# A hybrid attention/mLSTM decoder step: the rotary product of the query heads taken from TensorE to VectorE and GpSimd

## The reference

```python
def partial_rope(x, pos):
    half = ROT_DIM // 2                      # ROT_DIM = 32, half = 16
    ang = pos[:, None] * inv[None, :]
    cos, sin = jnp.cos(ang)[:, None, :], jnp.sin(ang)[:, None, :]
    x1, x2 = xf[..., :half], xf[..., half:ROT_DIM]
    return jnp.concatenate([x1 * cos - x2 * sin, x2 * cos + x1 * sin, xf[..., ROT_DIM:]], axis=-1)

aq = partial_rope(rms_norm(aq.reshape(B, S, ATT_HEADS, ATT_HD), q_norm_w), pos)
ak = partial_rope(rms_norm(ak.reshape(B, S, ATT_HEADS, ATT_HD), k_norm_w), pos)
```

## Time and profile before

| | |
|---|---|
| median of 3 runs | 468.84 us (468.48 to 469.5) |
| the profiled execution | 469.01 us, span 466.9 us |
| PE / PEld busy | 455.6 us (98%) / 414.0 us (89%) |
| DVE / ACT / POOL busy | 393.8 us (84%) / 290.5 us (62%) / 100.5 us (22%) |
| DMA | 150.91 MB, mean 323 GB/s |
| query stage on PE | about 17 us to 48 us of the span |

### The profile page before, as it was taken

The page is one execution under the profiler, slowest core; times in us unless marked ns, Lnnn a source line. Parts: engine busy times, 40 slices in busy tenths (PEclk is TensorE's granted clock), DMA queues, the critical chain, the costliest instruction groups (busy, mean ns, idle before and its releaser), DMA issues.

```text
span 466.9 us, 11342 instructions
## 1 busy us (share of the span) xinstructions
PE 455.6 (98%) x3855; PEld 414.0 (89%) x3855; DVE 393.8 (84%) x1610; ACT 290.5 (62%) x487; POOL 100.5 (22%) x181
## 2 busy tenths in 40 slices
PE   6999999999999999999999999999999999999997
PEld 4899899897879789888899889889898899899997
DVE  4898899699999799999899999889999946568861
ACT  4866545676984496896485695667958346324430
POOL 2040421013323213422321242312222201000000
PEclk9999999999999999999999999999999999999999
DMA  8899699749999999999999999998999995447511
GB/s 306 324 355 406 173 349 363 237 156 336 320 416 408 388 360 352 412 412 408 409 384 297 405 413 409 411 384 285 403 415 410 409 382 182 162 149 261 181 49 48
DMA packets 44858, 150.91 MB, mean 323 GB/s; under 512 B 6192, under 2 KB 7796, under 8 KB 44672
## 3 DMA queue, kind: packets, MB, share of 16 engines
q1 hardware_dynamic: 20368, 70.77, 41.0%
q0 software_dynamic: 19008, 67.20, 37.4%
q10 hardware_dynamic: 5424, 12.21, 6.9%
HBM read 137.37 MB, written 12.76 MB: 322 GB/s over the span
## 4 chain that ended last, share of the span: by engine, by line
PE 66%; ACT 12%; DVE 9%; DMA 7%; issue 4%; ACTq 1%; SPq 0%; DVEq 0%; POOLq 0%
PE pj L545 25%; PE pj L548 12%; PE wk L545 8%; PE pa L728 4%; PE wk L548 4%; DMA kpages<-in_cache_k 4%; ACT whi L829 3%; DVE kpages L1181 2%; DMA out_C_s<-cslot 2%; ACT L849 2%; DVE wlo L1082 2%; DVE cslot L1263 1%; PE wk L498 1%; PE wk L650 1%; PE wk L684 1%
## 5 line engine op out<-in xcount | busy, mean ns | idle before, releaser
L545 PE MATMUL pj<-xn,whi 128*128 128x264 f32 x1328 | 180.8, 289 | 1.6 <-ACT mqT L987 1.3
L545 PEld LDWEIGHTS pj<-xn,whi 128*128 128x128 f32 x1328 | 168.5, 189 | 10.2 <-issue 6.2
L1082 DVE TENSOR_TENSOR wlo<-wraw,whi 128x1024 fp32r<-128x1024 f32 x112 | 136.2, 1219 | 9.5 <-ACT whi L829 9.1
L829 ACT ACTIVATE whi<-wraw 128x1024 fp32r<-128x1024 f32 x112 | 117.9, 1053 | 21.0 <-PE wk L548 13.5
L1181 DVE CUSTOM_DVE_ANT_0 kpages<-kpages,qbc 128x128 f32<-128x128 f32 x512 | 116.3, 292 | 3.5 <-DMA kpages<-in_cache_k 3.3
L548 PE MATMUL pj<-xn,wlo 128*128 128x264 f32 x664 | 93.9, 284 | 0.7 <-DVE wlo L1082 0.7
L548 PEld LDWEIGHTS pj<-xn,wlo 128*128 128x128 f32 x664 | 85.4, 188 | 1.1 <-DVE wlo L1082 1.1
L418 POOL DMA_DIRECT2D kpages<-in_cache_k x64 | 34.3, 536 | 167.4 <-DVE sco L1181 145.1
L418 POOL DMA_DIRECT2D vpages<-in_cache_v x64 | 33.9, 530 | 60.6 <-issue 38.4
L1181 DVE DVE_READ_ACCUMULATOR2_ANT sco<- 128x1 f32 x512 | 42.1, 82 | 0.0
L728 PE MATMUL pa<-vpages,prob 128*32 128x256 f32 x512 | 33.8, 384 | 1.9 <-ACT prob L887 1.9
(11 more groups left out here) (270 smaller groups left out, 609.5 us busy)
## 6 DMA issues: line engine op xcount, KB each, us to landing
wraw<-in_weights SPq DMA_DIRECT2D x112, 512.0 KB, 6.7
kpages<-in_cache_k POOLq DMA_DIRECT2D x64, 512.0 KB, 8.4
vpages<-in_cache_v POOLq DMA_DIRECT2D x64, 512.0 KB, 11.1
cslot<-in_states SPq DMA_DIRECT2D x16, 512.0 KB, 8.8
out_C_s<-cslot ACTq DMA_DIRECT2D x16, 512.0 KB, 8.1
xres<-in_tokens SPq DMA_DIRECT2D x1, 1056.0 KB, 5.6
out_k_p<-kT ACTq DMA_DIRECT2D x4, 256.0 KB, 10.0
out_v_p<-v_nat ACTq DMA_DIRECT2D x4, 256.0 KB, 5.1
```

Of the source, the lines that this page charges most:

```text
L545: mm(bank[:, 0:T], whi[:, q, k, :], src[:, g, k, :], start=(k == 0 and g == 0), stop=False)
L829: A(whi[:, n % WSPLIT], wraw[:, n % WRAW], ACT.Copy).then_inc(whi_ready, 1)
L1082: V.tensor_tensor(wlo[:, n % WRAW], wraw[:, n % WRAW], whi[:, n % WSPLIT], ALU.subtract).then_inc(wlo_ready, 1)
```

## The change

For the 8 query heads PE no longer multiplies with the permutation matrix. DVE swaps the two halves of the 32 rotated rows by a lane shuffle inside SBUF, multiplies them with the sine (whose sign now lies in the table), and adds the product of the head's 32 rows with the cosine, which POOL makes into `hT[:, 1]` and announces by the semaphore `scaled`. The last multiplication by 1/rms still runs over all 128 rows. Rows 32 to 127 are no longer touched by cosine and sum. The keys still go through `norm_sums` and `rope_norm`, with the sign moved from the matrix to the table.

POOL's stream is written in another order: the 11 pages are issued in twos between the eight cosine products, and the decay rows' write and read are placed behind the products of head 5 and head 6. PE's wait for the buffer pair is on `rs_ready` where it was on `q_ready`.

```diff
+SWAP = [(m + ROT // 2) % ROT for m in range(ROT)]
@@ gpsimd
-            pool.wait_ge(proj, 2)
-            for s in range(KSLOTS):
-                keys(s)
-            for s in range(VSLOTS - 1):
-                values(s)
-
-            pool.wait_ge(rows_ready, 1)
-            pool.dma_start(rows_dram, rows[:, :, :].rearrange("p a t -> p (a t)")).then_inc(row_put, 16)
-            pool.wait_ge(row_put, 16)
-            decay_rows(0)
+            pool.wait_ge(blank, 6)
+            pool.wait_ge(boot_r, 16)
+            for h in range(HEADS):
+
+                pool.wait_ge(evac, h + 1)
+                if h:
+                    pool.wait_ge(q_ready, h)
+                pool.tensor_tensor(hT[0:ROT, 1, :], qT[0:ROT, h, :], cos[0:ROT], ALU.mult).then_inc(scaled, 1)
+                if h in (1, 2):
+                    for s in range(KSLOTS // 2):
+                        keys(KSLOTS // 2 * (h - 1) + s)
+                if h in (3, 4, 5, 6):
+                    for s in range(2 * (h - 3), min(2 * (h - 2), VSLOTS - 1)):
+                        values(s)
+                if h == 5:
+                    pool.wait_ge(rows_ready, 1)
+                    pool.dma_start(rows_dram, rows[:, :, :].rearrange("p a t -> p (a t)")).then_inc(row_put, 16)
+                if h == 6:
+                    pool.wait_ge(row_put, 16)
+                    decay_rows(0)
             spread_rows(0)
@@ tensor
                     pe.wait_ge(evac, g + 1)
-                    if g == 0:
-                        pe.wait_ge(boot_r, 16)
                     if g >= 2:
-                        pe.wait_ge(q_ready, g - 1)
-                    norm_sums(wk[2 * (g % 2)], wk[2 * (g % 2) + 1], g % 2, qT[:, g, :])
+                        pe.wait_ge(rs_ready, g - 1)
+                    mm(wk[2 * (g % 2)][:, 0:T], ones, sq[:, g % 2, :], start=True, stop=True).then_inc(norm_ps, 1)
@@ vector
+            def rope_head(h):
+
+                x = qT[:, h, :]
+                ch.link(V.stream_shuffle(hT[0:ROT, 0, :], x[0:ROT], SWAP))
+                ch.step(V.tensor_tensor(hT[0:ROT, 0, :], hT[0:ROT, 0, :], sin[0:ROT], ALU.mult))
+                ch.join()
+                dve.wait_ge(scaled, h + 1)
+                ch.link(V.tensor_tensor(x[0:ROT], hT[0:ROT, 0, :], hT[0:ROT, 1, :], ALU.add))
+                dve.wait_ge(rs_ready, h + 1)
+                V.tensor_tensor(x, x, rs[:, h % 2, :], ALU.mult).then_inc(q_ready, 1)
@@
                 dve.wait_ge(boot_r, 16)
-                dve.wait_ge(norm_ps, h + 1)
-                dve.wait_ge(rs_ready, h + 1)
-                rope_norm(qT[:, h, :], rs[:, h % 2, :], wk[2 * (h % 2) + 1], q_ready)
+                dve.wait_ge(evac, h + 1)
+                rope_head(h)
@@ constants
-        c[m + half, C_ROT + m] = -1.0
+        c[m + half, C_ROT + m] = 1.0
-        c[s * half:(s + 1) * half, C_SIN:C_SIN + T] = np.sin(ang)
+        c[s * half:(s + 1) * half, C_SIN:C_SIN + T] = (2 * s - 1) * np.sin(ang)
```

More of the change, by code:

```diff
@@ L290, in build @@
         blank, blank_eye = sem("blank"), sem("blank_eye")
+        scaled = sem("scaled")
         xsq_act, xsq_dve, xn_ready = sem("xsq_act"), sem("xsq_dve"), sem("xn_ready")
```

## The result

The changed kernel takes 478.31 us (476.71 to 478.36, four runs) against 468.82 for the kernel before: 1.0196 times as long, 95% interval 1.0178 to 1.0213. The forecast was 474.4, range 469.3 to 478.5. The direction and the chain of waits held; the size was 9.5 us where 5.6 had been forecast. The time lies outside the forecast's own range, which ended at 476.3, and only 0.2 us inside the wider one, whose end was the price of rival 3.

A forecast was written before the change was run, and what follows sets the result against it. PE was taken to bound the query heads (98% busy, 3.81 us a head). Landing +4.0 and clock +1.6 gave +5.6 on 469.0, 474.6, less 0.2: 474.4 us; own range 469.3 to 476.3, wider to 478.5.

The forecast's parts named there:

- rival 3: Much slower: POOL's product near 2.4 us delays pages and the rows' write, +9.7 us, 478.5 us; chance 12%.
- The path: Before PE's transposes: rows' landing, two reads, last cosine product, sum and scaling in turn, transposes at 52.4 instead of 48.4.
- signs of being wrong: Rows landing in under 5 us, no PE wait before transposes, POOL products over 1.5 us, or body's end unmoved despite PE's pause.
- PE: Query heads on PE without permutation matmuls: period 3.36 us instead of 3.81, chunk 8 ending 3.15 us earlier, at 44.7.
- From landing to transposes: Behind the landing: reads 1.0 us, product 0.8, handovers 0.1, sum and scaling 0.43 each; landing 49.5, transposes 52.4.
- The landing itself: Decay rows' write on POOL's queue lands at 49.5 us, as late as before; bounds 45.0 and 51.2.
- 28.5 + 9 x 2.27: POOL's page queue: first page lands at 28.5, nine more 2.27 us apart, so the tenth at 48.9.
- its upper bound: POOL's page queue: weights' greater share slows a page to 2.46 us, so the rows land at 51.2.
- 22.6 + 4 x 3.36 + ...: POOL's stream: four head periods after head 0's end at 22.6; last page ahead issued 38.6, rows' write 39.4.
- the product: POOL's cosine product of a query head: 0.8 us, bounds 0.3 and 2.4, with room in the first heads.
- The clock: PE's clock falls in its 7.6 us pause before the transposes, making first matmuls slow: +1.6 us, bounds 0 and 2.
- The library: POOL's library choices before the products and the spreading: a long first call, about 6 us, given no more weight.

The follow-up runs named there:

- experiment 1: Changed kernel with the decay rows' write issued by ScalarE on its own queue after head 5: 469.80 us, ratio 1.0040 to the kernel before.
- experiment 6: Kernel before without PE's eight permutation matmuls of the query heads, queries left unrotated: 468.57 us, ratio 0.9991.
- experiment 8: Changed kernel with the cosine product made by DVE and POOL's stream as in the kernel before: 470.09 us, ratio 1.0031.
- experiment 11: Changed kernel with POOL's order and waits kept but no cosine products made: 474.84 us, ratio 1.0144.
- experiment 10: Changed kernel with rows' write on ScalarE's queue, reads behind all products, two product buffers, only seven pages between products: 470.31 us, ratio 1.0032.
- experiment 4: Changed kernel with 24 matmuls of zeros on PE before its wait for the last query head: 475.86 us, ratio 1.0161.
- experiment 12: Against the kernel before: DVE does the whole rotation, two heads a pass, no permutation matmuls on PE, rows' write on ScalarE's queue: 466.64 us, 0.9965.
- experiment 2: Changed kernel with the wait and reads of the decay rows behind all eight products, write still on POOL's queue: 475.24 us, ratio 1.0142.
- experiment 3: Changed kernel with the rows' write on ScalarE's queue and the wait and reads behind all cosine products: 470.47 us, ratio 1.0049.
- experiment 9: Changed kernel with the cosine product on DVE, POOL's stream as before, and rows' write on ScalarE's queue: 471.05 us, ratio 1.0057.

## Why the prediction was right, and where its size was off

**The path.** Right in every step from the landing on: the rows' landing, the reads, the product, the sum, the scaling and the transposes stand in the chain in that order, and experiment 1 gives 7.3 us of the loss back by moving one write to another queue. Of the prediction's signs of being wrong one came true as well: products on POOL over 1.5 us.

**PE.** Right: the heads stand 3.36 us apart, and chunk 8 ended at 45.2 where 44.7 was forecast.

**From landing to transposes.** Forecast 2.9 us, measured 57.03 - 53.93 = 3.1. The last product is 0.75 us for a forecast 0.8.

**The landing itself** is the term that was too small: 53.9 for 49.5. The forecast worked it out from the pages ahead of the write: the first lands at 28.5, nine more follow at 2.27 us each, the write 0.6 later. The time of the write's issue (39.4) does not enter; that the write took 10.2 us where 49.5 - 39.4 = 10.1 is a coincidence. What the changed kernel shows for the first page (issued at 24.94) and for the ninth and tenth together (issued at 42.6 and 43.2):

```profile
DMA to landing us min/median/max: 5.2/5.2/5.2
DMA to landing us min/median/max: 9.1/9.8/10.5
```

The first page landed at 30.1, the tenth at 53.7, the write 0.2 later. That is 2.62 us a page, and in the terms of the forecast +1.6 for the first page, +3.2 for the pace and -0.4 for the write. The step that failed is "28.5 + 9 x 2.27", above all the pace.

Two things made the pages slower, and no run tells their shares apart. One needs nothing of POOL's new stream: with the stream of before and PE's heads at 3.36 us, the eleven pages landed 2.46 us apart in experiment 6 and 2.59 in experiment 8, where the kernel before had 2.27, and the write landed at 51.7 and 52.4. The forecast had this as its upper bound (2.46 us a page, by the weights' greater share) and took the old pace all the same. The other is that the new stream gives the queue its pages too late to keep it full. The stretch of 32 to 36 us, changed kernel, against the earlier trace rows:

```profile
32.00:36.00 4.00, 4.00 (x34) 3.93 (x33) 3.65 (x8) 3.15 (x7) 2.45 (x3) 1.00 0.93 322
```

322 GB/s stand here for 413. The pages are late because each pair is issued behind the end of a head on DVE, and so is the write, 43.7 for 39.4. The step behind that, "22.6 + 4 x 3.36 + ...", put the end of head 4 at 36.0; it came at 40.7. It had two faults.

First, the period. I let the heads go through POOL and DVE at PE's pace of 3.36 us. Between heads 0 and 3 DVE has the gates' operations to do besides, and it was full already in the kernel before: head 0 finished there at 23.9, head 4 at 39.2 (its L1123 starts at 38.81), 15.3 us and not 13.4. PE's own pace there, 4 x 3.81 = 15.2, hides this; but DVE's rows between the two show a single idle time, of 0.24 us, and in experiment 6, with PE's heads 3.36 us apart, the same four heads took 15.3 us again (L1123 starts at 23.88 and 39.23). Experiment 11 shows it without any product: head 4 at 39.1, 3.1 us of the 4.7 (0.7 of it at head 0 already, which ended at 23.3). I had read PE's rows of that stretch and not DVE's.

Second, the product. I gave it 0.8 us and cost it only on POOL. In experiment 10 and in the changed kernel it has that size when DVE is at nothing that shuts it out; but POOL is released by the end of DVE's head, and that is just when DVE starts its split of 1.2 us. So seven of eight products took 1.4 to 2.8 us, and stretched DVE's next operation by 0.56 us three times. This is the other 1.6 us of head 4's delay. Together with the last product's own time this is 2.4 us of the result (experiment 11), of which the forecast had the last product's 0.8. That the stated range held is luck in part. Rival 3 had the right sort of mechanism, a long product that delays pages and write, for another reason than the one I gave; its price of 478.5 is the time measured, though it is made of other terms (1.7 us beside DVE and not 2.4, and no longer last product).

The Trainium skill has this exclusion: "SBUF — State Buffer", section "SBUF: two separate sides", calls the port pair of VectorE and GpSimd "an exclusive lock, not a bandwidth split", taken by a VectorE operation with two SBUF inputs against a GpSimd operation that reads SBUF. The traces here agree: 1.71 against 0.78 us for the product, 1.32 against 0.68 for DVE's scan of two inputs, and the shuffle, with one input, was not stretched. L1151 has one input and was; the page names VectorE's 2-port modes as well, and no run here shows in which mode L1151 ran. The prediction set the skill's price of the product beside its own 0.8 us and passed over this rule, which bears on what the product meets on DVE.

**The clock.** Forecast +1.6 us, measured 1.5 to 1.6 (experiment 4), on a pause of 11.8 us instead of 7.6. Reading it off PE's slow start at 1.54 us was sound. In experiment 1 the clock fell around a pause of 4.03 us too, while in experiment 12 it stayed at 1.00 through one of 1.24 us.

**The library.** I gave no weight to a long first call since none showed in the kernel before. A silence of that size does show here, 5.77 us before L449, and DVE waited 2.3 us behind it. Experiment 11 shows that it comes with the products. In the changed kernel it is off the path: without it the transposes start 2.4 us earlier and the time is 2.4 us shorter (1.96 - 1.44%), so the silence cost nothing besides. In experiment 2 it was on the path, with the landing.

**The sum** in the terms of the prediction: +4.0 forecast for the landing is 4.0 + 4.4 (landing) + 0.2 (steps after it) = 8.6; +1.6 for the clock is 1.5; 10.1 in all, of which 0.4 is made good later on, so that the span is 9.7 longer.

## What to carry to other kernels

Before work goes to an idle engine, look at what else stands in that engine's stream and queue: a wait that nobody paid for becomes everybody's as soon as another engine waits for something behind it. Pace a loop by the slowest engine in it, read from that engine's own rows. Price a queue's backlog by its pace under the new load, not the old one. And cost a GpSimd operation on two inputs together with the VectorE operation that will run beside it. A saving on the busiest engine shows only if the next event that it runs into, here a landing that stood behind pages in a queue, moves as well.

## What the runs showed of the hardware that was not expected

- A GpSimd product of 32 x 264 takes 0.75 us alone, 1.7 us when it starts just behind the start of a VectorE split of 1.22 us, and VectorE's next operation on 4 partitions grows from 0.28 to 0.84. Where the product came first, VectorE's scan of two inputs grew from 0.68 to 1.32 (experiment 10).
- With the DMA engines at a share of about 1, a write of 8 KB landed in about 6 us on a queue with nothing else in it, and in 10.2 us (changed kernel), 14.3 (before) and 17.9 (experiment 8) behind pages of 512 KB on its own queue.
- Between its last two-tile product and a partition broadcast GpSimd was silent for 5.8 us in the changed kernel; without the products the same place took 1.2 us.
- The clock of TensorE was granted at half around each of the long pauses at the transposes, from 3.63 us (experiment 10) to 11.8 us (changed kernel). From the transposes to L565's like it then took 5.7 us (changed kernel, experiments 3, 8 and 9), and 6.9 in experiment 10, for 4.26 at the full clock (experiment 4). Through a pause of 1.24 us it stayed at 1.00 (experiment 12); behind a wait of 1.94 us at 59.4 us in experiment 6 it was 0.57.
